# Expert stage of a mixture-of-experts step: ScalarE rounds all weights, VectorE forms all low parts, GpSimd only moves rows, the down projection runs one step behind

## The reference, cut to what matters

```python
def ec_moe(h, w_router, w_gate, w_up, w_down):   # 16 experts, 2816 wide, model width 1024
    ...
    gates, idx = lax.top_k(aff.T, cap)           # each expert picks its tokens
    xs = ht[idx]                                 # gather: 128 latent + 32 context rows an expert
    a = jnp.einsum('ecd,edf->ecf', xs, w_gate)
    u = jnp.einsum('ecd,edf->ecf', xs, w_up)
    y = jnp.einsum('ecf,efd->ecd', jax.nn.silu(a) * u, w_down) * gates[..., None]
    out = out.at[idx.reshape(-1)].add(y.reshape(-1, d))      # scatter with addition
```

## Time and profile before

| what | value |
|---|---|
| median of three runs | 3482.92 us |
| span of the profiled execution (first to last instruction) | 3480.6 us |
| TensorE busy with matmuls | 3166.9 us, 91% |
| VectorE busy | 2532.4 us, 73% |
| GpSimd busy | 1483.4 us, 43% |
| ScalarE busy | 1278.2 us, 37% |
| mean granted TensorE clock | 0.949 |
| expert stage, from the first gate matmul to the last result in PSUM | about 883 to 3431 us |

### The profile page before, as it was taken

The page is one execution under the profiler, slowest core; times in us unless marked ns, Lnnn a source line. Parts: engine busy times, 40 slices in busy tenths (PEclk is TensorE's granted clock), DMA queues, the critical chain, the costliest instruction groups (busy, mean ns, idle before and its releaser), DMA issues. The chain is left out here.

```text
span 3480.6 us, 50738 instructions
## 1 busy us (share of the span) xinstructions
PE 3166.9 (91%) x19191; PEld 2741.1 (79%) x19191; DVE 2532.4 (73%) x3014; ACT 1278.2 (37%) x2046; POOL 1483.4 (43%) x860
## 2 busy tenths in 40 slices
PE   8999989894899999989898999999898989999994
PEld 2699987683788888878787888888787878888883
DVE  2343331225789898988898898989898989889895
ACT  2222221232334434434343344343434343434432
POOL 2233330123345455453545454544535354535443
PEclk9999999996899999999999999999999999999997
DMA  7311102344667676776767676767667576767673
GB/s 303 114 37 36 38 14 74 117 147 151 205 220 247 210 233 214 223 223 212 238 211 240 221 231 217 236 215 234 220 210 245 195 255 205 245 224 226 218 237 134
DMA packets 483305, 668.23 MB, mean 192 GB/s; under 512 B 14689, under 2 KB 418993, under 8 KB 480050
## 3 DMA queue, kind: packets, MB, share of 16 engines
q1 hardware_dynamic: 476978, 644.45, 55.6%
q0 software_dynamic: 6144, 20.98, 2.5%
HBM read 633.39 MB, written 31.98 MB: 191 GB/s over the span
## 5 line engine op out<-in xcount | busy, mean ns | idle before, releaser
L1202 POOL TENSOR_TENSOR wD_lo<-rawW,wD_hi 128x1024 fp32r<-128x1024 f32 x352 | 960.3, 2759 | 1162.7 <-DVE wD_hi L1541 1162.7
L1401 PE MATMUL psU<-X,wU_hi 128*128 128x320 f32 x2816 | 784.7, 360 | 93.1 <-DVE wU_lo L1202 93.1
L1401 PE MATMUL psG<-X,wG_hi 128*128 128x320 f32 x2816 | 760.9, 352 | 38.2 <-issue 35.1
L1202 DVE TENSOR_TENSOR wU_lo<-rawW,wU_hi 128x1024 fp32r<-128x1024 f32 x350 | 741.2, 2125 | 0.0
L1403 PE MATMUL psU<-X,wU_lo 128*128 128x160 f32 x2816 | 685.0, 243 | 0.0
L1403 PE MATMUL psG<-X,wG_lo 128*128 128x160 f32 x2816 | 677.7, 241 | 0.0
L1401 PEld LDWEIGHTS psU<-X,wU_hi 128*128 128x128 f32 x2816 | 552.7, 196 | 98.6 <-DVE wU_lo L1202 51.0
L1401 PEld LDWEIGHTS psG<-X,wG_hi 128*128 128x128 f32 x2816 | 543.7, 193 | 62.9 <-issue 41.7
L1403 PEld LDWEIGHTS psU<-X,wU_lo 128*128 128x128 f32 x2816 | 562.9, 200 | 0.0
L1403 PEld LDWEIGHTS psG<-X,wG_lo 128*128 128x128 f32 x2816 | 552.5, 196 | 6.4
L1202 DVE TENSOR_TENSOR wG_lo<-rawW,wG_hi 128x1024 fp32r<-128x1024 f32 x350 | 454.6, 1336 | 56.9 <-ACT wG_hi L1208 56.9
(11 more groups left out here) (239 smaller groups left out, 4213.0 us busy)
## 6 DMA issues: line engine op xcount, KB each, us to landing
rawW<-in_w_gate SPq DMA_DIRECT2D x176, 1024.0 KB, 7.4
rawW<-in_w_up SPq DMA_DIRECT2D x176, 1024.0 KB, 8.2
rawW<-in_w_down SPq DMA_DIRECT2D x176, 1024.0 KB, 4.9
wm<-in_w_mod SPq DMA_DIRECT2D x24, 1024.0 KB, 5.0
raw<-in_w_in SPq DMA_DIRECT2D x32, 192.0 KB, 2.4
rawc<-catT SPq DMA_DIRECT2D x10, 512.0 KB, 6.0
acc<-x SPq DMA_DIRECT2D x10, 512.0 KB, 2.7
xn<-xn SPq DMA_DIRECT2D x10, 512.0 KB, 4.1
```

Of the source, the lines that this page charges most:

```text
L1202: eng.tensor_tensor(lo, src, hi.bitcast(F32), ALU.subtract).then_inc(f_lo[kind], 1)
L1401: pe.matmul(out[:, f, 0:2 * C], hi, X[:, k, :], start=(k == 0), stop=False, skip_group_check=True)
```

## The change

- The rounding of the down weights moves from VectorE (the cast at L1541) to ScalarE, as its two last instructions of a step, behind the rounding of `hid`. Their subtraction moves from GpSimd to VectorE, as its last two instructions of a step.
- GpSimd keeps the gather and the scatter. The scaling of an expert's result moves to VectorE (`take_y`, in step 0 of the next expert, from PSUM directly); ScalarE keeps one of its three copies (`take_context_lo`).
- `wD` and `hid` get one buffer instead of two. ScalarE therefore waits for `down(i - 1)` before it writes `hid` and `wD_hi` of step i.
- The last `down` of an expert moves into step 0 of the next, behind G(0) and U(0); only the last expert appends its own.
- The transposes move from steps 3 to 10 to steps 2 to 9, and the scaling of the transposed rows (`x_mod`) moves from VectorE to ScalarE, where it stands ahead of `ul`. The rounding of `X` stands ahead of that of the up weights, and its subtraction ahead of `hf`.
- Both halves of `wG_lo` and `wU_lo` always follow one another on VectorE.

Cut to its core:

```diff
-            wD = [sb(f"wD_{x}", [P, 2, 2, D], F32R, c) for x in ("hi", "lo")]
+            wD = [sb(f"wD_{x}", [P, 2, D], F32R, c) for x in ("hi", "lo")]
-            hid = sb("hid", [P, 2, 2, 2 * C], F32R, c)
+            hid = sb("hid", [P, 2, 2 * C], F32R, c)
+            X_AT = 2
...
                 @block.tensor
-                    def down(e, i):
-                        pe.wait_ge(f_hl, 1 + s + 1)
-                        if i == 0:
-                            pe.wait_ge(f_y, e + 1)
+                    def down(e, i, first):
+                        pe.wait_ge(f_hl, s + 1)
+                        if i == 0 and not first:
+                            pe.wait_ge(f_y, e)
...
                             if i:
-                                down(e, i - 1)
-                        down(e, STEPS - 1)
+                                down(e, i - 1, first)
+                            elif not first:
+                                down(e - 1, STEPS - 1, False)
+                        if last:
+                            down(e, STEPS - 1, False)
...
                 @block.scalar
+                            if X_AT <= i < X_AT + NK and not last:
+                                x_mod(i - X_AT, 0).then_inc(f_xm, 1)
                             act.activation(ul[:], psU[:, :, C:2 * C], ACT.Copy).then_inc(f_ul, 1)
-                            if not end:
-                                hi_halves(act, U_, *n, halves=(0,) if i == STEPS - 1 else (0, 1))
-                            act.wait_ge(f_hf, s + 1)
-                            act.activation(hid[:, i % 2, :, 0:C], hf[:], ACT.Copy).then_inc(f_hh, 1)
                             if i == STEPS - 1 and not last:
                                 x_hi(e + 1)
-                                hi_halves(act, U_, *n, halves=(1,))
+                            if not end:
+                                hi_halves(act, U_, *n)
+                            act.wait_ge(f_hf, s + 1)
+                            if i or not first:
+                                act.wait_ge(f_d, s)
+                            act.activation(hid[:, :, 0:C], hf[:], ACT.Copy).then_inc(f_hh, 1)
+                            hi_halves(act, D_, e, i)
                             if i == 0 and not first:
-                                take_y(e)
+                                take_context_lo(e)
...
                 @block.vector
-                    def down_hi(e, i, s):
-                        dve.wait_ge(f_d, s + (1 if i else 2))
-                        raw_ready(dve, D_, e, i)
-                        for half in range(2):
-                            dst, src = split_part(D_, i, half, 0)
-                            dve.tensor_copy(dst, src).then_inc(f_hi[D_], 1)
+                    def take_y(e):
+                        dve.wait_ge(f_d, STEPS * e)
+                        dve.wait_ge(f_si, e)
+                        dve.scalar_tensor_tensor(ys[0][:]..., psS[:], gc[:, 0:1], gates[1][:, 0, :]..., ALU.mult, ALU.mult)
+                        dve.wait_ge(f_yp, e)
+                        dve.tensor_tensor(ys[1][:]..., psP[0:CP], yp[:]..., ALU.add).then_inc(f_y, 1)
+                        dve.wait_ge(f_y, e)
+                        dve.scalar_tensor_tensor(ys[1][:], ys[1][:], gc[0:CP, 1:2], gates[1][0:CP, 1, :],
+                                                 ALU.mult, ALU.mult).then_inc(f_ys, 1)
...
+                            for half in range(2):
+                                lo_half(dve, D_, e, i, half)
+                            if i == 0 and not first:
+                                take_y(e)
...
                 @block.gpsimd
                     def body(e, first, last):
-                        for i in range(STEPS):
...
-                            for half in range(2):
-                                lo_half(gp, D_, e, i, half)
-                            if i == 0 and not first:
-                                finish_context(e)
-                            if i == 1 and not first:
-                                scatter(e)
+                        if not first:
+                            scatter(e)
+                            gp.sem_inc(f_free, 1)
```

More of the change, by code:

```diff
@@ L1193, in split_part @@
             if kind == D_:
-                dst = wD[part][:, i % 2, half, :]
+                dst = wD[part][:, half, :]
             else:
@@ L1462, in _, with x_mod @@
                 def _(act):
-                    act.sem_inc(f_y, 1)
+                    def x_mod(k, bank):
+                        src = psU[:, bank, XT]
+                        for r, a, b in ((0, 0, CS), (1, CS, C)):
+                            op = act.activation(xm[:, k, a:b], src[:, a:b], ACT.Identity, bias=modT[:, 3, k, r:r + 1],
+                                                scale=scaleA[:, 1, k, r:r + 1])
+                        return op
                     def x_hi(e):
@@ L1559, in body @@
-                            if final:
-                                down_hi(e, i, s)
-                            for half in range(1 if final else 2):
-                                if not end:
+                            if not end:
+                                for half in range(2):
                                     lo_half(dve, G_, *n, half)
-                            if not final:
-                                down_hi(e, i, s)
                             dve.wait_ge(f_ul, s + 1)
@@ L1567, in body @@
                             dve.tensor_tensor(ua[:], psU[:, :, 0:C], ul[:], ALU.add).then_inc(f_ua, 1)
+                            if i == STEPS - 1 and not last:
+                                x_lo(e + 1)
                             dve.wait_ge(f_ua, 1 + s + 1)
                             dve.wait_ge(f_sg, s + 1)
-                            dve.wait_ge(f_hl, s + 1)
                             dve.tensor_tensor(hf[:], sg[:], ua[:], ALU.mult).then_inc(f_hf, 1)
                             if not end:
-                                if final:
-                                    lo_half(dve, G_, *n, 1)
-                                else:
-                                    for half in range(2 if i == 0 else 1):
-                                        lo_half(dve, U_, *n, half)
+                                for half in range(2):
+                                    lo_half(dve, U_, *n, half)
@@ L1582, in body @@
                             op.then_inc(f_hl, 1)
-                            if i >= STEPS - NK and not last:
-                                x_mod(i - (STEPS - NK), 0).then_inc(f_xm, 1)
-                            if final and not last:
-                                x_lo(e + 1)
-                            if not end and i:
-                                for half in range(0 if final else 1, 2):
-                                    lo_half(dve, U_, *n, half)
+                            for half in range(2):
+                                lo_half(dve, D_, e, i, half)
@@ L1591, in _ @@
+                            if i == 0 and not first:
+                                take_y(e)
                     experts(dve, body)
                     for_scatter(E)
-                    dve.wait_ge(f_y, 1 + E)
-                    dve.tensor_tensor(ys[1][:], ys[1][:], yp[:], ALU.add).then_inc(f_tail, 1)
-                    dve.tensor_tensor(ys[0][:], ys[0][:], gates[1][:, 0, :], ALU.mult)
-                    dve.wait_ge(f_tail, 1)
-                    dve.scalar_tensor_tensor(ys[1][:], ys[1][:], gc[0:CP, 1:2], gates[1][0:CP, 1, :],
-                                             ALU.mult, ALU.mult).then_inc(f_tail, 1)
+                    take_y(E)
@@ L1610, in gather, with scatter @@
                                                   ).then_inc(f_got, 16)
[L1612 to L1619 removed]
+                    def scatter(e):
+                        waits(gp, (f_ys, e))
                         for r, n in ((0, CS), (1, CP)):
```

95 lines of the change are left out of this document (34 added, 61 removed).

## The result

The changed kernel takes 3369.61 us (median of 4 runs, 3366.03 to 3372.44), the kernel before on the same chip 3484.18 us (4 runs). The ratio is 0.967, with a 95% interval of 0.9656 to 0.9683. The forecast was 3323 us with a range of 3295 to 3352: the direction was right, the time lies outside the range.

The account below looks back on a forecast made before the run. TensorE's own work was taken to set the pace, leaving its waits and low clock to win. 3480.6 - 157.6 + 2 = 3325 us, counted otherwise 3318; 3321 taken for the span, so 3323 us, range 3295 to 3352.

Parts of the forecast that it names:

- GpSimd's subtraction goes: VectorE's step: without GpSimd's contention, weight subtractions take 1.22 us each, `hf` about 0.5; step 9.4 of 12.89 us.
- ScalarE takes the down rounding: ScalarE's step: two halves cost 2.00 us, the step 8.7 of 12.89 us, none on the path; charged zero.
- One buffer: Single `hid` and `wD`: ready about T + 4.1, wanted at T + 8.3; costs nothing, with 4 us of cover.
- T + 4.1: T is the end of a `down` and TensorE's step; VectorE's two down subtractions end about 4.1 us later.
- The moved `down`: TensorE's steps 0 and 1 and expert's end: up-weight and `hid` waits, restarts and low clock go, 157.6 us.
- What stays: TensorE's loop branch: 13 "issue" waits remain with restarts and low clock, 13 x (2.70 + 0.17 + 1.56) = 57.6 us.
- The rim: Stage's start and end: last `down` waits about 3.0 us, 6.6 us behind it become 4.0; +2 us for all.
- Loads: SyncE's weight loads: down load waits some 7 us later, gate and up queue behind it; nothing charged.
- the branch also gets cheaper: Rival, 9%: at the loop's branch, low clock goes (3303 us), or half the wait too (3285 us).
- A new wait in step 1: Rival, 11%: `take_y` behind the down subtractions delays the first `down`; 15 experts lose 56 us, 3379 us.
- Slower: Rival, 3%: VectorE becomes the bound because long subtractions are not GpSimd's doing; step 15.5 us, 3660 us.
- does not do what it says: Rival, 2%: waits go but return elsewhere because single buffers chain the engines; the same 3480 us.

Follow-up runs that it names:

- The first experiment: Changed kernel with 48 already satisfied waits (24 instructions) added to TensorE's program ahead of the expert stage, moving the loop's head: 3330.37 us, ratio 0.9551.
- the second experiment: Kernel before the change with 430 already satisfied waits (215 instructions) added in the same idle stretch of TensorE: 3571.09 us, ratio 1.0242.
- the last experiment: Changed kernel with TensorE's experts written out, plus two unused GpSimd subtractions a step beside VectorE's for the up weights: 3329.98 us, ratio 0.9563.

## Why the prediction was wrong, and where it was right

*GpSimd's subtraction goes*: right in every number (1.22 and 0.49 us; GpSimd busy for 86 us in the stage, forecast under 120). The Trainium skill's rule that it weighed, page "SBUF — State Buffer", section "Who interferes with whom", holds in both directions: the up subtraction has a mean of 1221 ns without GpSimd beside it and 2228 ns with it.

*ScalarE takes the down rounding* and *One buffer*: right where the `down` is moved, no wait. The time that was given for the two halves, T + 4.1, shows where the cover is lost (the `down` at its old place): waits of 2.9 us for the first half and 0.7 for the second.

*The moved `down`*: right. Both waits, 93.1 and 8.3 us, went with their restarts and low clock. Without its loop term the forecast is 3323 - 57.6 = 3265 us; the kernel without the loop takes 3262.6.

*What stays*: this step failed. It took the 13 waits of the kernel before over unchanged, because the branch is the same and stands behind a `down` just as long. Measured were 107 us (3369.6 - 3262.6) instead of 57.6. TensorE's timelines at the 13 ends say where the difference lies: from the last matmul of the `down` to the first of U(0) it takes 12.49 us in the mean, before the change 8.95, together 46 us more. Of these, 33 are the second wait, which the earlier trace rows did not have (2.84 us from the first to the second product of G(0), before 0.27); 6 are the longer first wait (3.54 to the first product, before 3.09); and 7 are the longer low clock (6.11 for the rest of G(0), before 5.59). The first experiment shows that the second wait comes from the place of the loop's head in its packet, the second experiment that the kernel before pays for it as well once its head stands there. No step of the change asked for it; it shifted the head by 41 instructions. The term's form was wrong: it read the price of a branch as one of the wait in front of it, where it also depends on what lies behind its target. The prediction's own sign of being wrong here, a branch wait changed by more than 1 us, did not come: the first wait moved by 0.44 us, and the loss stood one instruction later.

*The rim*: the last `down` waited 2.9 us, forecast 3.0. From the last `down` to the span's end 47.0 us pass, before 49.2; forecast was 2.6 less. *Loads*: no wait of TensorE for them, right.

*The rivals*: "the branch also gets cheaper" had the right place and the wrong sign. "A new wait in step 1" did not come in the changed kernel, but the last experiment shows that its mechanism is real, at 67 / 15 = 4.5 us an expert where it was priced at 3.7. "Slower" and "does not do what it says" did not come either; that the long subtractions are GpSimd's doing, which the former doubted, the last experiment shows. The range was too narrow: it allowed the branch 1 us either way and gave no row for it.

What a page adds: the Trainium skill, page "Runtime: NRT & Kernel Launch", section "Instruction fetch mechanics", says that instructions come in 16 KiB blocks of 256, that a taken branch out of the window in hand has to fetch its target's block, and that crossing a block's boundary is mostly hidden. The packets of 16,384 bytes and the first wait agree. The last part holds in the kernel without the loop, and not right behind a branch, where the measurement decides: 2.4 us with 8 instructions left in the block, 5.2 us in the kernel before.

The size of the first wait, 2.70 before and 3.14 after, is not settled. That weight loads lengthen it is shown; but the DMA engines moved no more in the changed kernel from a branch's start to its packet's, at one end each (358 GB/s from 1777.99 to 1782.50, in the kernel before 394 from 1831.25 to 1835.10), so why its packet starts later stays open.

## What to carry to other kernels

A long loop on the engine that sets the pace can have a price at each end that no instruction of the body shows; here a body of 1942 instructions had it and one of 1327 had not. Look for waits that end in "issue" at the body's first and second instruction, and write the loop out on that engine alone where the program has room. Where the loop must stay, keep its head away from the end of an instruction packet, and when an edit changes the code ahead of the loop, expect the place to move and the time with it. And a forecast that keeps a wait "because nothing about it changes" should price it from what makes it, not from its row.

## What the runs showed of the hardware

- 215 instructions that do nothing, ahead of a loop, made a kernel 2.4% slower; 24 of them made another 1.2% faster (3369.6 to 3330.4).
- The taken branch of the experts' loop (1942 instructions) takes 7.0 us on TensorE beside full weight loads and 3.4 us beside an eighth of them; that of a loop of 1327 instructions, in an earlier stage, 0.21 to 0.24 us, with no instruction packet.
- One GpSimd subtraction of 128x1024 floats takes 2.39 us in the mean where it slows VectorE's gate subtractions and 3.31 beside its up subtractions, and VectorE's 1.22 become 1.49 and 2.23.
- Not every wait lowers the clock: in the kernel before without its loop an expert has three waits for `wU_lo` (2.81, 1.06 and 3.61 us) and one stretch at 0.50, of 6.83 us, around the end of the last of them. The window (columns as in the earlier trace rows):

```profile
1853.94:1860.77 6.83, 5.90 (x21) 5.41 (x22) 6.13 (x8) 2.21 (x4) 6.25 (x3) 0.50 0.89 251
```
